# Gate and up projections of a SwiGLU FFN by a two by two block scheme with seven products

## The reference

```python
def rms_norm(x, w):
    xf = x.astype(jnp.float32)
    xf = xf * lax.rsqrt(jnp.mean(xf * xf, axis=-1, keepdims=True) + EPS)
    return (xf * w.astype(jnp.float32)).astype(x.dtype)
...
def swiglu(h, w_gate, w_up, w_down):
    return (jax.nn.silu(h @ w_gate) * (h @ w_up)) @ w_down
...
        h = h + swiglu(rms_norm(h, ffn_norm_w[i]), ffn_w_gate[i], ffn_w_up[i], ffn_w_down[i]).astype(h.dtype)
```

## Time and profile before

| | us |
|---|---|
| median of three runs | 1462.07 (1460.95 to 1462.79) |
| the profiled execution, its own time | 1461.54 |
| span of its trace | 1459.7 |
| gate and up stages, first and second FFN | 241.2 and 241.3 |
| down stages, first and second FFN | 119.7 and 123.3 |

### The profile page before, as it was taken

The page is one execution under the profiler, slowest core; times in us unless marked ns, Lnnn a source line. Parts: engine busy times, 40 slices in busy tenths (PEclk is TensorE's granted clock), DMA queues, the critical chain, the costliest instruction groups (busy, mean ns, idle before and its releaser), DMA issues.

```text
span 1459.7 us, 19487 instructions
## 1 busy us (share of the span) xinstructions
PE 1443.1 (99%) x7346; PEld 1187.3 (81%) x7346; DVE 832.2 (57%) x1147; ACT 611.5 (42%) x998; POOL 253.6 (17%) x278
## 2 busy tenths in 40 slices
PE   9999999999999999999999999999999999999999
PEld 7878888788888888888888877777888888888887
DVE  4797787854644444333487756789544544444231
ACT  5477676644322222222233356778314322222121
POOL 4323423103000000000000018766103000000000
PEclk9999999999999999999999999999999999999999
DMA  9201010221322322322232233333132232232322
GB/s 341 87 30 59 1 59 30 87 81 65 106 96 86 112 90 89 112 102 99 87 116 87 86 132 116 115 102 110 65 115 87 87 108 94 86 115 87 115 86 86
DMA packets 23342, 139.19 MB, mean 95 GB/s; under 512 B 2672, under 2 KB 3440, under 8 KB 8944
## 3 DMA queue, kind: packets, MB, share of 16 engines
q1 hardware_dynamic: 20544, 127.54, 24.5%
q10 hardware_dynamic: 2736, 10.81, 2.1%
HBM read 136.18 MB, written 2.16 MB: 95 GB/s over the span
## 4 chain that ended last, share of the span: by engine, by line
PE 90%; DVE 3%; ACT 3%; issue 1%; POOL 1%; DMA 1%; SPq 0%; ACTq 0%; POOLq 0%; DVEq 0%
PE ps L491 23%; PE ps L493 23%; PE ps L492 23%; PE ps L850 4%; PE ps L1034 3%; PE ps L828 2%; PE ps L808 2%; PE ps L1086 1%; PE ps L717 1%; PE ps L752 1%; ACT seg L1441 1%; PE ps L753 1%; DVE sm L1823 1%; PE ps L1077 1%; PE ps L824 1%
## 5 line engine op out<-in xcount | busy, mean ns | idle before, releaser
L1571 DVE TENSOR_TENSOR wl<-wraw,wh 128x2048 fp32r<-128x2048 f32 x109 | 250.7, 2300 | 238.9 <-ACT wh L1131 238.9
L491 PE MATMUL ps<-xh,wh 128*128 128x512 f32 x896 | 351.6, 392 | 0.0
L493 PE MATMUL ps<-xh,wl 128*128 128x512 f32 x896 | 348.9, 389 | 0.0
L492 PE MATMUL ps<-xl,wh 128*128 128x512 f32 x896 | 348.8, 389 | 0.0
L1131 ACT ACTIVATE wh<-wraw 128x2048 fp32r<-128x2048 f32 x109 | 208.0, 1909 | 181.8 <-PE ps L493 180.4
L493 PEld LDWEIGHTS ps<-xh,wl 128*128 128x128 f32 x896 | 168.2, 188 | 35.4
L491 PEld LDWEIGHTS ps<-xh,wh 128*128 128x128 f32 x896 | 168.2, 188 | 35.2 <-issue 0.7
L492 PEld LDWEIGHTS ps<-xl,wh 128*128 128x128 f32 x896 | 168.3, 188 | 35.0 <-issue 0.7
L492 PE MATMUL ps<-hl,wh 128*128 128x512 f32 x352 | 136.9, 389 | 0.0
L493 PE MATMUL ps<-hh,wl 128*128 128x512 f32 x352 | 136.9, 389 | 0.0
L491 PE MATMUL ps<-hh,wh 128*128 128x512 f32 x352 | 136.9, 389 | 0.0
(11 more groups left out here) (311 smaller groups left out, 2382.7 us busy)
## 6 DMA issues: line engine op xcount, KB each, us to landing
wraw<-wstream SPq DMA_DIRECT2D x111, 1024.0 KB, 4.7
rowc<-cum_rows ACTq DMA_DIRECT2D x16, 512.0 KB, 3.6
cw<-cw_in SPq DMA_DIRECT2D x1, 4096.0 KB, 14.1
xT<-xT_in SPq DMA_DIRECT2D x8, 256.0 KB, 6.1
part<-xT_in ACTq DMA_DIRECT2D x1, 2048.0 KB, 10.7
out<-xT SPq DMA_DIRECT2D x8, 256.0 KB, 6.5
wraw<-wstream SPq DMA_DIRECT2D x2, 512.0 KB, 8.2
wraw<-wstream SPq DMA_DIRECT2D x3, 256.0 KB, 5.2
```

The lines of the kernel that those rows point to most:

```text
L491: mm(o, wa[0], xa[0], start=start, stop=False)
L492: mm(o, wa[0], xa[1], start=False, stop=False)
L493: return mm(o, wa[1], xa[0], start=False, stop=stop)
L1571: TTo(wl[:, s, :], wraw[:, s, :], wh[:, s, :].bitcast(F32), ALU.subtract).then_inc(lo_done, 1)
```

## The change

Of the eleven gate and up chunk pairs of each FFN the first three (`PLAIN`) stay as they are. The other eight make four pairs of pairs (`PAIRS`), each of two *units*, one for gate and one for up (`UNITS` = 8). A unit takes two gate chunks (or two up chunks), 512 output features, and sees x as a 2 x 2 matrix of blocks (512 input features x 256 tokens) and the weights as a 2 x 2 matrix of blocks, each a half chunk of 4 input tiles x 256 features. It makes the four result blocks from seven block products in place of eight (the form with 15 additions). A block product is 2 x 4 `split_product`s of 256 tokens: 24 matmuls of 256 columns.

The x operands of the seven products, four of them sums of blocks (`s1` to `s4`) of x normalized in full (`xn`, 8 operations on DVE), are made once per FFN in the plain turns, with high and low parts (`mix_hi`, `mix_lo`). The weight operands are made for each unit: four sums on DVE (`weight_sum`, partly in place), a cast of each of the seven on ACT (`pair_hi`) and its low part on DVE (`pair_lo`). They pass through four quarter slots in `wh` and `wl`; a slot is free when the product four before is done. The raw chunks of gate units are loaded into `wraw`, those of up units into a new buffer `wx`.

The seven sums of the results: PE adds products 3 and 5 onto product 1 in one bank (`y`), 4 onto 0 (`x`), 6 onto 2 (`z`). Between them ACT copies `x` after product 0 (`p1`), `y` after `y += p1` (`u2`) and `y` after product 3 (`u3`); DVE adds `p1` to `y` in place and subtracts `u3` from `z` (block 22) and, after product 6, `u2` from `z` (block 12, `v12`). PE waits for each of these before it writes that bank again; product 2 waits for `v12` of the unit before. ACT applies four Silus to a gate unit's blocks, DVE multiplies them with the up unit's into `later_hidden`, which lies where `xh` and `xl` were.

The high and low parts of all 22 hidden tiles are made later: tiles 0 to 5 (high) and 0 to 2 (low) within the last unit, the others after it, 8 to 21 behind the split of the second down chunk. Their places are those of the mixes and of the raw buffers. PE waits for each tile in the first half chunk of each output pair of the down stage.

```diff
+PLAIN = 3
+PAIRS = (FT // 2 - PLAIN) // 2
+PAIRED = 4 * PAIRS
+PARTS = 7
+UNITS = 2 * PAIRS
+MIXES = KT + 4
+OPERANDS = PARTS * (UNITS + 1)
...
+        mix_hi, mix_lo, mix_raw = [], [], []
+        for n in range(PARTS):
+            mix_hi.append(a.take(f"mix_hi{n}", [P, 4, 256], F32R))
+            mix_raw.append(nc.alloc_sbuf_tensor_at(f"mix_raw{n}", [P, 4, 256], F32, offset=a.end))
+            mix_lo.append(a.take(f"mix_lo{n}", [P, 4, 256], F32R))
...
+        def part_source(n0, u, idx):
+            return (raw_quarter(n0, u, 0, 0), wsum[:, :], raw_quarter(n0, u, 0, 0), raw_quarter(n0, u, 1, 0),
+                    raw_quarter(n0, u, 0, 1), wsum[:, :], raw_quarter(n0, u, 1, 1))[idx]
+        def part_slot(t, n0, u, idx):
+            q = (2 * (n0 % 2) + PARTS * u + idx) % 4
+            return t[:, q // 2, (q % 2) * 1024:(q % 2 + 1) * 1024]
...
+        def operand(f, u, idx):
+            return OPERANDS * f + PARTS * (u + 1) + idx
...
+            def paired_loads(f, n0):
+                source = n0 - 1 + f * PAIRED + 2 * PLAIN
+                for u in range(UNITS):
+                    for e in range(2):
+                        if u < 2:
+                            sp.wait_ge(lo_done, n0 + 2 * PLAIN)
+                        else:
+                            sp.wait_ge(part_lo, operand(f, u - 2, 6 + e))
+                        dst = wx[:, e, :] if u % 2 else wraw[:, (n0 + e) % 2, :]
+                        sp.dma_start(dst, wstream[source + 4 * (u // 2) + 2 * e + u % 2]
+                                     ).then_inc(up_landed[e] if u % 2 else gate_landed[e], 16)
+                for e in range(2):
+                    sp.wait_ge(part_lo, operand(f, UNITS - 2, 6 + e))
+                    ring_load(n0 + 2 * PLAIN + e, n0 - 1 + (f + 1) * PAIRED + 2 * PLAIN + e)
...
+            def pair_unit(f, n0, u):
+                U = UNITS * f + u
+                j0 = PARTS * U
+                x_bank, y_bank, z_bank = pair_banks(u)
+                def part_product(idx, bank, start):
+                    pe.wait_ge(part_lo, operand(f, u, idx) + 1)
+                    hi, lo = part_slot(wh, n0, u, idx), part_slot(wl, n0, u, idx)
+                    for m in range(2):
+                        for k in range(4):
+                            w = slice(k * 256 + m * P, k * 256 + (m + 1) * P)
+                            o = ps[:, bank, m * 256:(m + 1) * 256]
+                            x, xl_ = mix_hi[idx][:, k, :], mix_lo[idx][:, k, :]
+                            mm(o, hi[:, w], x, start=start and m + k == 0, stop=False, skip_group_check=True)
+                            mm(o, hi[:, w], xl_, start=False, stop=False, skip_group_check=True)
+                            ins = mm(o, lo[:, w], x, start=False, stop=k == 3, skip_group_check=True)
+                    ins.then_inc(part_mm, 1)
+                if u == 1:
+                    pe.wait_ge(evac, EVAC["up1" if f else "up0"] + 2 * PLAIN)
+                if u > 1 and u % 2 == 0:
+                    pe.wait_ge(act_done, 4 * (PAIRS * f + u // 2))
+                if u > 1 and u % 2:
+                    pe.wait_ge(h_done, 4 * (PAIRS * f + u // 2))
+                part_product(0, x_bank, True)
+                part_product(1, y_bank, True)
+                after(pe, unit_added, 3 * U)
+                part_product(2, z_bank, True)
+                pe.wait_ge(unit_copied, 3 * U + 2)
+                part_product(3, y_bank, False)
+                pe.wait_ge(unit_copied, 3 * U + 1)
+                part_product(4, x_bank, False)
+                pe.wait_ge(unit_copied, 3 * U + 3)
+                part_product(5, y_bank, False)
+                pe.wait_ge(unit_added, 3 * U + 2)
+                part_product(6, z_bank, False)
...
-                with pe.Fori(1, FT // 2 - 1) as i:
-                    turn(i)
-                hidden = FT * (1 + (L == 3))
-                pe.wait_ge(gate_in, hidden)
-                pe.wait_ge(hl_done, hidden - 4)
-                residual(down, hs, ready=lambda: pe.wait_ge(hl_done, hidden))
+                turn(2)
+                for u in range(UNITS):
+                    pair_unit(f, n0, u)
+                pe.wait_ge(gate_in, h0 + 2 * PLAIN)
+                residual(down, hs, each=lambda kt: pe.wait_ge(hl_done, FT * f + kt + 1))
...
+            def hidden_hi_tile(f, t):
+                if t < 2 * PLAIN:
+                    act.wait_ge(evac, EVAC["up1" if f else "up0"] + t + 1)
+                else:
+                    act.wait_ge(h_done, 4 * (PAIRS * f + (t - 2 * PLAIN) // 4 + 1))
+                last = PARTS * (UNITS * f + UNITS - 1)
+                if t < 17:
+                    act.wait_ge(part_mm, last + (t // 4 if t < 6 else (2 * t - 5) // 4) + 1)
+                else:
+                    act.wait_ge(part_lo, OPERANDS * (f + 1))
+                A(hidden_hi[t][:, :], raw_hidden(t), ACT.Copy).then_inc(hh_done, 1)
...
+            def pair_hi(f, n0, u, idx):
+                j = PARTS * (UNITS * f + u) + idx
+                if PARTS * u + idx < 4:
+                    act.wait_ge(products, 2 * (n0 + 2 * PLAIN - 1 + idx // 2))
+                else:
+                    act.wait_ge(part_mm, j - 3)
+                if idx in (0, 4, 6):
+                    act.wait_ge((up_landed if u % 2 else gate_landed)[idx == 6], 16 * (PAIRS * f + u // 2 + 2))
+                else:
+                    act.wait_ge(sum_done, 4 * (UNITS * f + u) + {1: 2, 2: 1, 3: 3, 5: 4}[idx])
+                A(part_slot(wh, n0, u, idx), part_source(n0, u, idx), ACT.Copy).then_inc(part_hi, 1)
...
+            def pair_unit(f, n0, u):
+                U = UNITS * f + u
+                j0 = PARTS * U
+                x_bank, y_bank, z_bank = pair_banks(u)
+                gate_unit, last = u % 2 == 0, u == UNITS - 1
+                pair_hi(f, n0, u, 1)
+                pair_hi(f, n0, u, 2)
+                if not gate_unit:
+                    pair_act(f, u - 1, 3)
+                act.wait_ge(part_mm, j0 + 1)
+                after(act, unit_added, 3 * U - 2)
+                A(p1[:, :], ps[:, x_bank, :], ACT.Copy).then_inc(unit_copied, 1)
+                pair_hi(f, n0, u, 3)
+                act.wait_ge(unit_added, 3 * U + 1)
+                after(act, unit_added, 3 * U)
+                A(u2[:, :], ps[:, y_bank, :], ACT.Copy).then_inc(unit_copied, 1)
+                pair_hi(f, n0, u, 4)
+                pair_hi(f, n0, u, 5)
+                act.wait_ge(part_mm, j0 + 4)
+                after(act, unit_added, 3 * U - 1)
+                A(u3[:, :], ps[:, y_bank, :], ACT.Copy).then_inc(unit_copied, 1)
+                pair_hi(f, n0, u, 6)
+                if not last:
+                    pair_hi(f, n0, u + 1, 0)
+                else:
+                    for t in range(2 * PLAIN):
+                        hidden_hi_tile(f, t)
+                    act.wait_ge(part_mm, j0 + 5)
+                    split_hi(n0 + 2 * PLAIN)
+                if gate_unit:
+                    for n in range(3):
+                        pair_act(f, u, n)
...
+            def weight_sum(f, n0, u, n):
+                made = 4 * (UNITS * f + u)
+                q11, q21 = raw_quarter(n0, u, 0, 0), raw_quarter(n0, u, 0, 1)
+                q12, q22 = raw_quarter(n0, u, 1, 0), raw_quarter(n0, u, 1, 1)
+                dst, one, two = ((q11, q11, q12), (wsum[:, :], q11, q22), (q12, q12, q22), (wsum[:, :], wsum[:, :], q21))[n]
+                if n == 0:
+                    dve.wait_ge((up_landed if u % 2 else gate_landed)[1], 16 * (PAIRS * f + u // 2 + 2))
+                if n == 1:
+                    dve.wait_ge(sum_done, made + 1)
+                TTo(dst, one, two, ALU.add).then_inc(sum_done, 1)
...
+            def v12(f, u):
+                U = UNITS * f + u
+                dst = differ[:, 1, :] if u % 2 else act_gate[:, 1, :]
+                dve.wait_ge(part_mm, PARTS * U + 7)
+                TTo(dst, ps[:, pair_banks(u)[2], :], u2[:, :], ALU.subtract).then_inc(unit_added, 1)
+                if u % 2:
+                    pair_hidden(f, u, 3)
+            def pair_unit(f, n0, u, begin):
+                U = UNITS * f + u
+                x_bank, y_bank, z_bank = pair_banks(u)
+                gate_unit, last = u % 2 == 0, u == UNITS - 1
+                begin()
+                pair_lo(f, n0, u, 1)
+                pair_lo(f, n0, u, 2)
+                weight_sum(f, n0, u, 2)
+                dve.wait_ge(part_mm, PARTS * U + 2)
+                dve.wait_ge(unit_copied, 3 * U + 1)
+                y = ps[:, y_bank, :]
+                TTo(y, y, p1[:, :], ALU.add).then_inc(unit_added, 1)
+                pair_lo(f, n0, u, 3)
+                pair_lo(f, n0, u, 4)
+                weight_sum(f, n0, u, 3)
+                pair_lo(f, n0, u, 5)
+                dve.wait_ge(unit_copied, 3 * U + 3)
+                TTo(act_gate[:, 3, :] if gate_unit else differ[:, 0, :], ps[:, z_bank, :], u3[:, :], ALU.subtract
+                    ).then_inc(unit_added, 1)
```

(103 more changed lines are left out.)

215 lines of the change are left out of this document (147 added, 68 removed).

## The result

The changed kernel takes **1439.1 us**, median of six runs (1438.05 to 1440.21), against 1462.38 (1460.95 to 1462.79) for the kernel before: ratio 0.984, 95% interval 0.983 to 0.985. The forecast was 1440.4. The profiled execution took 1438.24 us with a span of 1436.4.

The account below looks back on a forecast made before the run. PE, busy 99% of the span, was taken as the bound. Terms -25.6 + 2.1 + 1.0 + 0.8 = -21.7 us against the profiled 1461.54 gave 1439.8, so 1440.4 us for the median; range 1428 to 1457.

Parts of the forecast that it names:

- The pairs: Gate and up units of both FFNs: 256-column matmuls every 120 ns, 16 units saving 1.60 us each, -25.6 us.
- A: Matmuls in the units come at the cadence of weight loads, 113 ns, kernel 1427 us; chance 0.10.
- B: Weight load not covered in the units, 134 ns per 256-column matmul, kernel 1475 us; chance 0.08.
- B2: No overlap of weight load and stream in the units, 228 ns per matmul, kernel 1726 us; chance 0.01.
- The border: From up unit to next gate unit, three per FFN: PE waits for DVE's low part, 0.35 us each, +2.1 us.
- x mixes: Scalings, sums, casts and low parts of x on DVE and ACT beside the plain pairs: cost nothing.
- First unit: Start of the first unit: low part 1 late by a few tenths, +1.0 us for both FFNs, bounds 0 and 3.
- Hidden tiles: Start of the down stage: PE follows DVE's making of hidden low parts with a lag, +0.8 us for both FFNs.
- Rival C: DVE becomes the bound in the units, 1.73 us per 1024-wide operation as beside POOL, kernel 1473 us; chance 0.03.
- mild form: DVE's operations in the units at 1.3 us or longer hand-overs, late operands at each border, 1448 us; chance 0.10.

Follow-up runs that it names:

- The first kernel of the experiments: The kernel before, with each 512-column matmul of the looped pairs done as two of 256 with the same weights: 1480.5 us, ratio 1.013.
- The edit that moves it: The changed kernel with DVE making the low part of operand 1 ahead of `v12` of the unit before: 1437.34 us in a single run.
- the run with quarters: The kernel before, with each 512-column matmul of the looped pairs done as four of 128: 1758.98 us in a single run.
- the first edit at the down start: The changed kernel with the first down chunk split after two hidden tiles and tiles 2 to 5 made behind it: 1437.58 us in a single run.
- the kernel with the additions in up units: The changed kernel with one more 1024-wide DVE addition at the end of up units 1, 3 and 5 of each FFN: 1446.44 us, ratio 0.989.
- the last version: The changed kernel with operand 1's low part and the down split moved earlier, hidden tiles 6, 7 before `v12`, up unit's first loads one chunk earlier: 1437.05 us.

## Why the prediction was right

*The pairs, -25.6:* right. Steps of 0.120 us, 2 x (161.28 - 174.05) = -25.5. The first kernel of the experiments gets the same step without the scheme, so it is the width that costs. The row that the figure was taken from was thinner than the prediction had it: of the three 256-wide matmuls in a chain before 102.48 the third has bf16 operands, so two steps of this number format carried it, and the figure held over 2688. Rivals A (113 ns) and B (134 ns) fall, A's floor showing at 128 columns only, and so does B2 (228 ns). By the estimate from the Trainium skill ("TensorE: Matmul & The Clock Gate", section "Back-to-back issue gap"), 109 ns, the saving would have been 38 us; the trace has 0.120 and does not agree.

*The border, +2.1:* right in place, count and releaser, too large in size: 0.13 us each, 0.8 in all. The step that was mis-sized is DVE's queue, added up from 1.17 and 0.69 us per operation. Successive operations start 1.14 and 0.60 to 0.71 us apart, so the low part ends some 0.2 us sooner than the sum has it; the 0.35 had been rounded upward besides. The edit that moves it takes back just 0.13 per border.

*x mixes, 0:* right, 67.16 us against 67.18 for the first FFN's plain pairs.

*First unit, +1.0:* too large, 0.04 us each. The assumption about loads held in the first FFN, where the first landed 4.7 us after its issue, and was the weak part in the second: there it took 5.3 to 7.5 us from profile to profile, and in two profiles the first unit waited 0.5 and 0.8 us for it. In the changed kernel's own profile it took 6.1 and came in time.

*Hidden tiles, +0.8:* wrong in its first half. I took PE's first wait to be for a hidden tile; it was for the low part of the first down chunk's weights, a step I hadn't costed (0.6 per FFN). The wait for tile 3 is there too, 0.4 per FFN. Together 2.0. I'd counted the 22 subtractions and only the *next-but-one* split behind them, not the split that the down stage's first matmul needs.

*Sum:* -25.5 + 0.8 + 0.1 + 2.0 = -22.6 us against the forecast's -21.7. Three small terms were off by -1.3, -0.9 and +1.2 and partly cancelled, which is luck: the good total says nothing for them. The two profiled executions are 23.3 us apart; the rest of that, some 0.6 us, lies outside the FFNs, where profiles of one and the same kernel differ by more.

*Rival C:* rightly held off by POOL's rest; its mild form didn't come either. Its full price, 1473 against 1440.4, was 16 us for each FFN and too low: with POOL at work beside little more than half of one FFN's units it was 26. The prediction took 1.73 us an operation, the run has 2.06, and the clock fell as well.

## What to carry to other kernels

A matmul of this format at the 2.4 GHz level costs its columns over the clock plus 14 ns that do not shrink, and under some width a cadence that no longer falls with the columns. Here seven eighths of the columns gave 59% of the eighth (25.5 of 43.5 us), because the 14 ns ride on 168 matmuls in place of 96. The same scheme with 128 columns would lose outright, at 0.112 us a matmul (an estimate from the run with quarters). An engine's reserve isn't its idle share but the reserve at the place in its queue: at 79% busy the same extra operation was free in one place and cost all of itself in another. When a wait is removed, look at what stands next in the same queue before booking the gain: the first edit at the down start took away 1.0 us of waits per FFN and got 0.7 back as a wait at tile 6.

## What the runs showed of the hardware that was not expected

The 14 ns over the columns at 2.4 GHz are the same whether successive matmuls use different weights or, as in the pairs of the first experiment, the same ones loaded again (0.120 us in both). At the 1.2 GHz level they don't show: 256-column matmuls start 0.213 us apart (twelve steps in 2.56 us, from 490.84 to 493.40; the rows below are the first), which is the columns alone. What the 14 ns are stays open.

Waits of PE went with a lower granted clock. With a third of the matmuls out, PE waited 0.7, 0.9, 0.9 and 2.4 us within 16 us before the clock fell at 490.4; it was 0.96 over 40 us. With POOL busy it fell within a wait of 4.40 us and was 0.83 over 20 us. The changed kernel, with waits of 0.6 us and less in these stages, has 1.00 throughout them, and so has the kernel with the additions in up units, whose waits of 1.0 us come three to an FFN.

```profile
490.46 0.58 PE L745 MATMUL ps<-mix_hi,wh 128*128 128x256 f32 x1 [2.44 <-DVE wl L1884]
490.84 0.41 PE L746 MATMUL ps<-mix_hi,wl 128*128 128x256 f32 x1
491.05 0.41 PE L745 MATMUL ps<-mix_hi,wh 128*128 128x256 f32 x1
```

So a wait there costs more than its own length.

A load's time to landing differs by place. Four loads of 1 MB are issued in a row ahead of the first unit in both FFNs of the changed kernel. The first of them landed after 4.7 us in the first FFN and after 6.1 in the second; over the profiles it is 4.6 to 4.9 and 5.3 to 7.5. With only two in a row (the last version) it was 5.8 in the second FFN, so their number is not the reason. What is stays open.
